# A complex state scan with fewer operations a step, and expert matmuls in another order: two layers on eight cores

## The reference

```python
def linear_scan(lam_bar, bu):                 # h[t] = lam_bar * h[t-1] + bu[t], complex
    a = jnp.broadcast_to(lam_bar, (1,) + bu.shape[1:])
    _, h = lax.associative_scan(_linear_combine, (a, bu), axis=1)
    return h
...
    for direction in range(2):                # s5_mixer: 32 groups x 64 complex states
        h_c = linear_scan(lam_bar, bu_c)      # context first
        bu = bu.at[:, 0].add(lam_bar * h_c[:, -1])
        h = linear_scan(lam_bar, bu)          # then the latent tokens, from its last state
...
    # hier_moe: weights is zero but for two of 16 experts of each token
    gate = jnp.einsum('bsd,edf->bsef', h, w_gate)
    up = jnp.einsum('bsd,edf->bsef', h, w_up)
    act = jax.nn.silu(gate) * up * weights[..., None].astype(h.dtype)
    return jnp.einsum('bsef,efd->bsd', act, w_down)
```

## Time and profile before

| | us |
|---|---|
| median of 4 runs | 7480.74 |
| lowest and highest | 7446.85 and 7564.94 |
| the profiled execution | 7458.93 |
| its span, on core 3, the slowest | 7457.4 |
| its shortest core | 7422.4 |

### The profile page before, as it was taken

How to read it: one execution, slowest core, us unless ns; L and a number is a source line. 1 busy time by engine, 2 the same in 40 slices (tenths; PEclk the granted TensorE clock), 3 DMA queues, 4 the chain that set the end, 5 groups by cost and what they waited for, 6 DMA issues and landing times.

```text
span 7457.4 us, 91411 instructions; the slowest of 8 cores (7422.4 to 7457.4 us)
## 1 busy us (share of the span) xinstructions
PE 4312.4 (58%) x27716; PEld 2712.7 (36%) x27716; DVE 3873.4 (52%) x9786; ACT 1258.5 (17%) x2090; POOL 1638.3 (22%) x1914
## 2 busy tenths in 40 slices
PE   4379995004464468888803599920074644888860
PEld 0278881004331243333302488820073214333320
DVE  0267771777333515555532577777763351455543
ACT  0223330000212121000012233300002212100001
POOL 0344441111110320000033344421112022101003
PEclk9678887557777669999955788865597765999975
DMA  7200003000212321111022000000002032212111
GB/s 186 75 6 2 1 1 136 1 1 2 68 29 65 102 71 56 53 52 52 22 89 97 7 1 1 1 1 1 1 8 91 1 118 74 79 51 68 51 40 73
DMA packets 180115, 342.03 MB, mean 46 GB/s; under 512 B 53984, under 2 KB 119776, under 8 KB 175328
## 3 DMA queue, kind: packets, MB, share of 16 engines
q1 hardware_dynamic: 134016, 236.98, 10.1%
q10 hardware_dynamic: 35584, 58.72, 2.4%
q0 software_dynamic: 10032, 40.47, 1.8%
HBM read 300.40 MB, written 45.19 MB: 46 GB/s over the span
## 4 chain that ended last, share of the span: by engine, by line
PE 45%; DVE 27%; issue 9%; DMA 6%; POOL 5%; ACT 4%; DVEq 1%; another core or an unknown queue 1%; SPq 1%; ACTq 0%; POOLq 0%
PE ps L241 41%; DVE arena L213 22%; PE ps L245 4%; POOL arena L213 4%; ACT arena L232 2%; DVE arena L248 2%; DMA arena<-xs 2%; DVE arena L222 2%; DMA arena<-w_mod 1%; ACT arena L236 1%; DVEq L139 1%; DMA arena<-w_o 1%; POOL arena L251 1%; DVE arena L492 1%
## 5 line engine op out<-in xcount | busy, mean ns | idle before, releaser
L241 PE MATMUL ps<-arena 128*128 128x64 bf16 (+6 forms) x25676 | 3887.4, 319 | 1965.3 <-DVE arena L213 1413.1
L241 PEld LDWEIGHTS ps<-arena 128*128 128x128 bf16 (+2 forms) x25676 | 2376.9, 116 | 3474.1 <-issue 2792.7
L213 DVE TENSOR_TENSOR arena<-arena 128x16 f32<-128x16 f32 (+6 forms) x6296 | 1476.1, 272 | 1216.9 <-DMA arena<-xs 288.7
L213 DVE TENSOR_TENSOR arena<-arena,ps 128x512 f32<-128x512 f32 (+3 forms) x1956 | 1272.9, 667 | 1194.3 <-PE ps L241 1119.9
L245 PE MATMUL ps<-arena 128*128 128x128 f32 (+2 forms) x2040 | 439.9, 382 | 952.8 <-POOL arena L213 671.7
L213 POOL TENSOR_TENSOR arena<-arena 128x1024 f32<-128x1024 f32 (+1 forms) x214 | 530.4, 2481 | 2090.0 <-DVE arena L213 1532.3
L238 POOL CAST arena<-arena 128x64 bf16<-128x64 f32 (+1 forms) x682 | 340.9, 500 | 2529.3 <-PE ps L241 1386.6
L248 DVE TENSOR_TENSOR_SCAN arena<-arena 128x512 bf16<-128x512 f32 (+1 forms) x640 | 678.5, 1120 | 154.8 <-ACT arena L236 154.8
L238 POOL COPY arena<-arena 128x64 bf16<-128x64 bf16 (+3 forms) x742 | 565.1, 766 | 872.0 <-DVE arena L248 728.6
L245 PEld LDWEIGHTS ps<-arena 128*128 128x128 f32 (+2 forms) x2040 | 345.4, 205 | 1043.2 <-issue 1042.1
L236 ACT COPY arena<-ps 128x512 f32<-128x512 f32 (+3 forms) x862 | 472.3, 551 | 1127.7 <-PE ps L241 979.1
(11 more groups left out here) (16 smaller groups left out, 159.7 us busy)
## 6 DMA issues: line engine op xcount, KB each, us to landing
arena<-xs SPq DMA_DIRECT2D x174, 512.0 KB, 3.7
arena<-w_gate SPq DMA_DIRECT2D x32, 1024.0 KB, 5.4
arena<-w_up ACTq DMA_DIRECT2D x32, 1024.0 KB, 5.9
arena<-w_down SPq DMA_DIRECT2D x32, 1024.0 KB, 7.2
xs<-arena POOLq DMA_DIRECT2D x52, 512.0 KB, 3.7
arena<-w_mod SPq DMA_DIRECT2D x16, 1536.0 KB, 7.0
arena<-w_mod ACTq DMA_DIRECT2D x16, 1536.0 KB, 7.0
arena<-modv SPq DMA_DIRECT2D x32, 512.0 KB, 7.5
```

The source lines that it names most:

```text
L213: S.op(eng, lambda e: e.tensor_tensor(out=out_, in0=a, in1=b, op=op), reads, writes)
L241: S.op('pe', lambda e: e.matmul(out_, lhsT=lhsT, rhs=rhs, start=start, stop=stop), reads, writes)
```

## The change

The diff has two parts, one for each stage, and 1000 more columns of the arena for their tiles.

In the scan the state lies in a ring RING of 16 slots of 64 columns, in two halves of eight. A step has four operations on VectorE, all of 128x64: CA = z * LRR, CB = (z with real and imaginary part swapped, read through a step of -1) * LIS, where LIS holds the imaginary part of lam as (-, +), CA = CA + x, and z' = CA + CB into the next slot. After every eighth step ACT copies the eight states of a half into XZ.

In the expert stage the down matmuls of a block become a generator, down_pairs, and exp_U takes two pairs of the block before it after each group of eight gate or up matmuls. The activations have two tiles, ACTTs3, which alternate from block to block, and the three banks of the pairs are counted on from block to block. load_expert for the next expert is issued behind the first block of an expert. After the last block its eight pairs stand alone.

```diff
-            ZP = [alloc(64), alloc(64)]
-            CAB = alloc(128)
...
-                for h in range(2):
...
-                    TT(CH_E, cab, zp3[:, us, :].unsqueeze(2).to_broadcast([128, 16, 2, 2]), LL4v[:, us], ALU.mult,
-                       [zpk + 'r', zpk + 'i', 'LL4'], [ck])
-                    TT(CH_E, cab[:, :, 0, :], cab[:, :, 0, :], xk, ALU.add, [ck, 'XZ'], [ck])
-                    TT(CH_E, zn3[:, us, 0], cab[:, :, 0, 0], cab[:, :, 1, 1], ALU.subtract, [ck], [znk + 'r'])
-                    TT(CH_E, zn3[:, us, 1], cab[:, :, 0, 1], cab[:, :, 1, 0], ALU.add, [ck], [znk + 'i'])
-                nk = f'ZP{(k + 1) % 2}'
-                CP('pool', XZ4[:, :, k + 1, :], zn3, [nk + 'h0r', nk + 'h0i', nk + 'h1r', nk + 'h1i'], ['XZ' + str(k)])
+            NBC = 8
+            RING = alloc(2 * NBC * 64)
...
+            MEMSET('pool', RG4[:, 2 * NBC - 1], 0.0, ['ZZ'])
             for k in range(NCH):
+                sl = k % (2 * NBC)
+                zp3 = RG4[:, (sl - 1) % (2 * NBC)]; zn3 = RG4[:, sl]
+                hb = f'ZR{sl // NBC}'
+                xk = XZ4[:, :, k + 1, :]
+                TT(CH_E, CA3, zp3, LRR3, ALU.mult, ['ZZ', 'LRR'], ['CA'])
+                TT(CH_E, CB3, zp3[:, :, ::-1], LIS3, ALU.mult, ['ZZ', 'LIS'], ['CB'])
+                TT(CH_E, CA3, CA3, xk, ALU.add, ['CA', 'XZ'], ['CA'])
+                TT(CH_E, zn3, CA3, CB3, ALU.add, ['CA', 'CB'], ['ZZ'] + ([hb] if sl % NBC in (0, NBC - 1) else []))
+                if sl % NBC == NBC - 1:
+                    CP('act', XZ4[:, :, k + 2 - NBC:k + 2, :], RG4[:, sl + 1 - NBC:sl + 1].rearrange("p s u c -> p u s c"), [hb], ['XZ' + str(k)])
...
+            def exp_U(e_, bi, par, gen, n):
...
+                for fc in range(2):
+                    for kc in range(8):
+                        MM(PS[fc][:, 0:ntok], WGa3[:, kc, fc * 128:(fc + 1) * 128], H2T3[:, kc, tok0:tok0 + ntok], kc == 0, kc == 7,
+                           [f'WGa{wp}', 'H2T'], [f'ps{fc}'])
+                    ACT(SIL[fc][:, 0:ntok], PS[fc][:, 0:ntok], AF.Silu, [f'ps{fc}'], [f'SIL{fc}'])
+                    take(gen, n)
+                    for kc in range(8):
+                        MM(PS[2 + fc][:, 0:ntok], WUp3[:, kc, fc * 128:(fc + 1) * 128], H2T3[:, kc, tok0:tok0 + ntok], kc == 0, kc == 7,
+                           [f'WUp{wp}', 'H2T'], [f'ps{2 + fc}'])
...
+                    TT('dve', SIL[fc][:, 0:ntok], SIL[fc][:, 0:ntok], PS[2 + fc][:, 0:ntok], ALU.mult,
+                       [f'SIL{fc}', f'ps{2 + fc}'], [f'SIL{fc}'])
+                    TT('dve', at3[:, fc, 0:ntok], SIL[fc][:, 0:ntok], PS[4][:, 0:ntok], ALU.mult,
+                       [f'SIL{fc}', 'ps4'], [f'ACTT{par}{fc}'])
+                    take(gen, n)
+                take(gen, 8)
...
+            for ix, (e_, bi) in enumerate(items_x):
+                exp_U(e_, bi, ix % 2, gen_x, 2)
+                if bi == 0 and e_ + 1 < NE:
+                    load_expert(e_ + 1)
+                gen_x = down_pairs(e_, bi, ix % 2)
+            take(gen_x, 8)
```

More of the change, by code:

```diff
@@ L177, in build_nc @@
         S.debug = dbg
-        ARENA_COLS = 50000
+        ARENA_COLS = 51000
         arena = st.enter_context(nc.sbuf_tensor("arena", [128, ARENA_COLS], F32))[:]
@@ L658, in build_nc @@
+            RG4 = r4(RING, 32, 2)
+            LIS = alloc(64); LIS3 = r3(LIS, 2)
+            TS('dve', LIS3[:, :, 0], LII3[:, :, 0], -1.0, None, ALU.mult, None, ['LII'], ['LIS'])
+            CP('dve', LIS3[:, :, 1], LII3[:, :, 1], ['LII'], ['LIS'])
+            CA = alloc(64); CB = alloc(64)
+            CA3 = r3(CA, 2); CB3 = r3(CB, 2)
+            MEMSET('pool', RG4[:, 2 * NBC - 1], 0.0, ['ZZ'])
             CH_E = 'dve'
             for k in range(NCH):
-                zp = ZP[k % 2]; zn = ZP[(k + 1) % 2]
@@ L1027, in build_nc, with down_pairs @@
             ACTT = alloc(2 * 512, BF16); ACTT3 = r3(ACTT, 512)
+            ACTTs3 = [ACTT3, r3(alloc(2 * 512, BF16), 512)]
+            dcount = [0]
+            def down_pairs(e_, bi, par):
+                wp = e_ % 2
+                WDn3 = r3(WDn_[wp], 1024)
+                tok0, ntok = blocks_F[bi]
+                at3 = ACTTs3[par]
+                for i in range(ntok // 128):
+                    ti = tok0 // 128 + i
+                    for hf in range(2):
+                        pb = 5 + dcount[0] % 3
+                        dcount[0] += 1
+                        for fc in range(2):
+                            MM(PS[pb], at3[:, fc, i * 128:(i + 1) * 128], WDn3[:, fc, hf * 512:(hf + 1) * 512], fc == 0, fc == 1,
+                               [f'ACTT{par}{fc}', f'WDn{wp}'], [f'ps{pb}'])
+                        fk = f'FACC{ti}'
+                        if e_ == 0:
+                            CP('act', FACC3[:, ti, hf * 512:(hf + 1) * 512], PS[pb], [f'ps{pb}'], [fk])
+                        else:
+                            TT('dve', FACC3[:, ti, hf * 512:(hf + 1) * 512], FACC3[:, ti, hf * 512:(hf + 1) * 512], PS[pb], ALU.add,
+                               [f'ps{pb}', fk], [fk])
+                        yield
@@ new lines, in take @@
+            def take(gen, n):
+                for _ in range(n):
+                    next(gen, None)
+            def exp_U(e_, bi, par, gen, n):
+                wp = e_ % 2
+                WGa3 = r3(WGa_[wp], 256); WUp3 = r3(WUp_[wp], 256)
+                tok0, ntok = blocks_F[bi]
+                at3 = ACTTs3[par]
+                for fc in range(2):
+                    for kc in range(8):
[6 more added lines that the diff above has]
+                           [f'WUp{wp}', 'H2T'], [f'ps{2 + fc}'])
+                    if fc == 0:
+                        MM(PS[4][:, 0:ntok], SEL3[0:32, e_, :], RWT[0:32, tok0:tok0 + ntok], True, True, ['SEL', 'RWT'], ['ps4'])
+                    TT('dve', SIL[fc][:, 0:ntok], SIL[fc][:, 0:ntok], PS[2 + fc][:, 0:ntok], ALU.mult,
[4 more added lines that the diff above has]
+                take(gen, 8)
@@ L1028, in build_nc @@
+            items_x = [(e_, bi) for e_ in range(NE) for bi in range(len(blocks_F))]
             load_expert(0)
[L1029 to L1032, removed]
+            gen_x = iter(())
+            for ix, (e_, bi) in enumerate(items_x):
+                exp_U(e_, bi, ix % 2, gen_x, 2)
+                if bi == 0 and e_ + 1 < NE:
                     load_expert(e_ + 1)
[L1034 to L1061, removed]
```

6 lines of the change are left out of this document (removed).

## The result

The changed kernel takes 6751.74 us (median of 11 executions, 6636.88 to 6948.31) where the kernel before takes 7499.79 (median of 16, 7445.55 to 7620.44). The ratio is 0.8882, 95% interval 0.8834 to 0.893: faster, within the range and 48 us under the forecast. (The ratio leaves out executions in which half of the chip had a lower clock for long, so it isn't the quotient of the medians.) The profiled execution took 6707.31 us, with a span of 6705.8 on core 7. Its cores 0 to 5 ended after 6613 to 6648 us; only cores 6 and 7 were longer.

A forecast was written before the change was run, and what follows sets the result against it. It took scan latency and TensorE and VectorE taking turns in the experts as the bounds. From 7458.9 us it subtracted 428 for the scans and 234 for the experts: 6797, so 6800, range 6700 to 6900, chance 0.41.

The forecast's parts named there:

- The scan step: Scan on VectorE: three dependent operations with gaps, 0.978 us a step, 285 us a layer, 428 us saved in all.
- The rival without overlap (1.197): Scan: VectorE does not overlap the two products, 1.197 us a step, 120 us more, 6917 in all; chance 0.06.
- The 512-token block: Expert stages: 49 matmuls without stalls, 10.83 us a block at full clock instead of 13.75, or 13.2 at 0.81.
- The bound of 12.9: Expert stages: down pairs still paced by VectorE's additions, 12.9 us a block, 6896 at full clock; chance 0.04.
- The short blocks: Layer 0 experts: 8.0 us for the 256-token block, 9.06 for the next, 49.6 an expert instead of 61.9.
- The moved loads: Expert stages: the next expert's weight loads, issued behind the first block, arrive in time and cost nothing.
- The 391 of the prediction: Both expert stages at full clock: 198 us saved in layer 0, 187 in layer 1, minus 4, plus 10.
- The full-clock sum: Whole kernel, rival: full clock throughout, 7458.9 - 428 - 391 = 6640 us; chance 0.25.
- The clock: Expert stages: slowest core spends half their time at 0.81, TensorE having no pauses; 234 us saved there.
- 0.81 throughout: Expert stages, rival: clock at 0.81 all the time, only 77 us saved there, 6954 us in all; chance 0.22.
- The slower rival: Expert stages: clock at 0.50, 21.1 us a block, 996 us more, 8027 in all; chance 0.02.

The follow-up runs named there:

- e3: Changed kernel with the scan's addition of x moved ahead of the second product; three executions 6711.44 to 6716.25 us, one 6760.53, ratio to the kernel before 0.8972.
- e5: Changed kernel with all eight down pairs issued behind the next block's first gate group; median 6823.19 us, ratio to the kernel before 0.9132.
- e1: Kernel before with the new scan alone, its expert stage unchanged; 7133.21 to 7208.74 us in four executions.
- e8: Changed kernel run once more without an edit; 6638.85 to 6734.96 us, ratio to the kernel before 0.8868.
- e7: Changed kernel with the experts' input H2T set to zero; 6649.35 to 6665.0 us, ratio to the kernel before 0.8888.
- e9: Changed kernel with the experts' input H2T set to zero, run again for more executions; 6650.87 to 6697.18 us, ratio to the kernel before 0.8925.
- e10: Kernel before with the experts' input set to zero; 7455.16 to 7496.61 us, ratio to the unedited kernel before 1.0005.
- e2: Changed kernel with the old scan put back, keeping the new expert order; median 7091.02 us, ratio to the kernel before 0.9465.
- e4: Changed kernel with layer 1's modulation spread through layer 0's scan and the ring cleared on VectorE; median 6621.24 us, ratio to the kernel before 0.8691.

## Why the prediction was right, point by point

- **The scan step.** Predicted 0.978 and 285 us a layer; measured 0.988 and 290.7. The operations of the chain are 6 ns longer than the products of the earlier trace rows and the gaps 3 ns shorter. With one more wait in eight steps and the irregular delays the mean is 290.7 / 288 = 1.009. Saved 416 instead of 428. The rival without overlap (1.197) fell: the second product starts 0.142 us behind the first. e3 shows the same from the other side: behind another operation it costs 0.134. In the Trainium skill (VectorE: DVE Perf Modes, The DRAIN you can't avoid) the sentence that held was the second, on an operation that is not held.
- **The 512-token block.** Predicted 10.83 at 1.00 and 13.2 at 0.81; measured 10.8 and 13.1. The bound of 12.9, pairs paced by their additions, was not met by the change. e5 shows that it was a real danger: with a burst of eight, four of them were paced, at 12.07.
- **The short blocks.** Predicted 8.0 and 9.06 for an expert's first two blocks; measured 7.6 and 9.06. The 256-token block was sized too long by 0.4 us: its limit was put on VectorE's 8.0, but VectorE's lag reaches TensorE only as one wait of 0.16, and the block stays near TensorE's own 7.2. An expert came out at 49.0 for 49.6. Both stages together saved 392 us at 1.00. The 391 of the prediction holds 10 for a full clock that these 392 don't, so the like figure is 381.
- **The moved loads.** Predicted free; in the waits of after TensorE waits for no DMA and no cast.
- **The full-clock sum.** 6640 was a rival's time, and the lowest executions are 6636.88, 6637.18 and 6638.14 us. Its working is thus right to a few us. Part of that is luck of signs: the scans were 12 us too optimistic (416 for 428), and the experts 11 too pessimistic (392 for 381).
- **The clock.** Here the forecast was right in kind and wrong in size and reason. It took half of the expert stages' time at 0.81 on the slowest core. In the profiled execution core 7 had 379 of some 1550 us, a quarter, and 379 x 3/16 = 71 us accounts for what lies between 6637 and 6707. The median stands (6751.74 - 6637) / 314 = 37% of the way to 0.81 throughout, by the prediction's own price of 391 - 77 = 314 us; which stages lost the time in executions without a profile isn't known. By medians the change saves 748 us where the forecast's sum has 662 (7458.9 - 6797). The reason given, that TensorE without pauses loses the clock, is not borne out. e1 loses it with pauses, e8 keeps it without, and e7, e9 and e10 show that the data decides whether it is lost at all. What the lack of pauses does is make each lost stretch dearer.
- **The slower rival** (0.50 in the expert stages) fell: no such stretch occurs in them.

## What to carry to other kernels

In a chain of small dependent operations count dependences, not operations: here one costs an operation plus 0.104 us, a wait more costs 0.069, and an operation beside the chain costs nothing. Look at the longest operations too, and not only at their mean: beside this chain one addition on POOL cost 6.5 us. Where two engines take turns inside a block, issue the second half of one block in small portions between the groups of the next, and spread them so that no bank is needed faster than it is emptied; the same pairs in one burst gave back 1.3 us a block of the 3 gained. Once TensorE sets the time, expect its clock to show in the spread of the times, and judge an edit by stretches at the same granted clock.

## What was unexpected of the hardware

- The granted clock fell to 0.81 on pairs of neighbouring cores, within 0.2 us in 16 of 17 falls, in before with the other six cores at 1.00 to the end of layer 1's experts, and it came back within one loop of matmuls (195 us at 1.00 between two stretches of 0.81 on core 3 of e2).
- TensorE without a pause and with the reference's data held 1.00 for 540 us on core 7 of after, and on all eight cores through both expert stages of e8.
- ACT's 512-element copy of eight states takes 638 ns and yet costs the scan only a longer wait, 0.17 instead of 0.104 us, in every eighth step.
- An addition on POOL over two partitions, 2x3072, held the VectorE operation that started under it for 6.48 and 6.65 us, where it takes 0.22 alone (e4, all cores).
